# First two units of a convolved feed-forward taken tile by tile, squares added on VectorE, one column sum inside the third unit

## The chip, the cores and the metric

One NeuronCore of one Trainium2 chip runs the kernel. The metric is the device time of one execution in microseconds (us); the median of three runs of the kernel before is 2436.14 us.

## What is computed

A sequence of 512 tokens of width 1024 goes through two blocks. The first has a feed-forward, a gated linear attention mixer, a cross attention and a second feed-forward. The second adds 16 meta tokens (528 rows in all) and has two layers: an attention mixer or a pooling mixer, each followed by a feed-forward with a convolution over tokens. The change touches only how these two convolved feed-forwards begin. Cut to that:

```python
def rmsnorm(x, g):
    xf = x.astype(jnp.float32)
    y = xf * lax.rsqrt(jnp.mean(xf * xf, axis=-1, keepdims=True) + NORM_EPS)
    return (y * g.astype(jnp.float32)).astype(x.dtype)

def conv_ffn(h, w_up, conv_w, conv_b, w_down):
    L = h.shape[1]
    u = h @ w_up
    up = jnp.pad(u, ((0, 0), (CONV_WIDTH - 1, 0), (0, 0)))
    u = conv_b + sum(conv_w[j] * up[:, j:j + L] for j in range(CONV_WIDTH))
    gate, val = jnp.split(u, 2, axis=-1)
    return (jax.nn.silu(gate) * val) @ w_down

    # in each of the two layers, m being the mixer's output:
    h = h + rmsnorm(m, norm_mix_post[i])
    f = conv_ffn(rmsnorm(h, norm_ffn_pre[i]), ffn_w_up[i], ffn_conv_w[i], ffn_conv_b[i], ffn_w_down[i])
    h = h + rmsnorm(f, norm_ffn_post[i])
```

## The kernel before, in words

**Layout.** Activations lie transposed: the width of 1024 is KD = 8 tiles of 128 partitions, and the tokens are columns. X holds the residual, M the output of a mixer or feed-forward (8 tiles of 528 columns, free once it has been added to X). A number is split for TensorE into a high and a low part (XHI and XLO; w_hi and w_lo for weights).

**Units.** All weights are a flat list of units, numbered through the program. A unit of a feed-forward's first matrix is one output tile: for each of the 8 input tiles three products (lines 549, 551, 553), each in two column halves of 264 (258 in the second layer, which works on 516 columns), summed in one of four pairs of PSUM banks, pair n mod 4. A unit passes four engines: SP loads it into one of RAW = 4 slots, ACT copies it to w_hi in two halves (line 495, act_hi), POOL subtracts to get w_lo in two halves (line 482), PE multiplies. There are only SPLIT = 2 slots of w_hi and w_lo, so ACT takes unit n+2 only after PE has summed unit n, and PE starts each half of a unit only when POOL has done it (lo_done).

**The order of work** is written out by hand, one program for each engine, and the engines meet at semaphores. Before each convolved feed-forward, cffn0 and cffn1, stands a step called post (dve_post, act_post): for each tile k VectorE scales M by gain and norm (line 971), adds it to X (line 975) and later computes XLO (line 649), ACT computes XHI (line 638) and the square of X (line 644) into one of two buffers sq. In the loop of dve_post the XLO of tile k-3 follows the scaling of tile k.

**The norm of the feed-forward** needs the sum over all 1024 rows of the squares. In the kernel before TensorE forms it: pe_first_unit runs the first unit one tile at a time, as XLO arrives, and after each tile multiplies the tile's squares with a matrix of ones (pe_square, line 571) into the free bank pair n+3. From the sum VectorE makes ms (line 693), ACT takes a logarithm and an exponential (lines 675 and 676, with a table load before each), VectorE refines them in three steps (680 to 682) into rn, and only then can it read the first unit out of PSUM (line 915).

**ACT's order at the start of a feed-forward** (act_ffn, up, with it = 0, a = 0) matters for what follows:

```python
                    soon = blk > 1 and first(it) and pi == 0 and a == 0
                    look(it, n, 2 * a, count)
                    if first(it) and pi == 0 and a == 0:
                        act_sqrt(act, s, w)
                    act.wait_ge(unit_read, later(n, it, 2 * a + 1))
                    ...
                        nc.scalar.activation(g_conv[:, 0:w], g_buf[:, 2:2 + w], ACT.Identity, scale=tap(inv - 2, 2, f),
                                             bias=tap(inv - 2, 3, f)).then_inc(conv_tap, 1)
                        if soon:
                            look(it, n, 2 * a + 1, count)
```

The first look prepares unit n+2. Then come the root, the wait until VectorE has read unit n, and the convolution's first tap (line 861); the second look, which prepares unit n+3, stands behind them. The text below counts the units of a feed-forward from 0: unit 0 and unit 1 are prepared before it starts, unit 2 by the first look, unit 3 by the second.

## Time and profile before

| what | value |
|---|---|
| time, three runs | 2435.87, 2436.14, 2441.85 us, median 2436.14 |
| profiled execution, first to last instruction (span) | 2434.0 us |
| profiled execution, its own device time | not listed; the median is 2.1 us above the span |
| PE busy | 2298.1 us (94%) |
| DVE, ACT, POOL busy | 1082.2 us (44%), 910.5 us (37%), 981.7 us (40%) |
| mean granted clock of TensorE | 0.975 of full speed |
| step post and start of cffn0 | from 1534 to 1579 us of the span |
| step post and start of cffn1 | from 2011 to 2055 us of the span |

Engines: PE is TensorE's matmuls, DVE VectorE, ACT ScalarE, POOL GpSimd. Times within the profile are us from the span's start. A row of a timeline gives start, length, engine, line, output and inputs, how many instructions it merges and, in brackets, how long the engine had been idle and who released it. A clock of 1.00 is 2.4 GHz and one of 0.50 is 1.2 GHz. One matmul of the program for the column sum of squares shows as two records.

### The profile page before, as it was taken

How to read it: one execution, taken by the hardware profiler on the slowest of the kernel's cores; microseconds unless marked ns; L12 is line 12 of the kernel's file. 1: busy time of each engine (PE TensorE's matmuls, PEld its weight loads, DVE VectorE, ACT ScalarE, POOL GpSimd, SP SyncE). 2: the span in 40 equal slices, each digit the busy share in tenths (PEclk: the TensorE clock that was granted, in tenths of full speed). 3: DMA queues.
4: the chain of work that ended last, by engine and by line, in shares of the span. 5: the costliest groups of instructions: out<-in, count | busy, mean ns of one | idle time of the engine just before them, and what ended most of it. 6: DMA issues, size and time to landing. Idle time of an engine off the chain costs nothing.

```text
span 2434.0 us, 35964 instructions
## 1 busy us (share of the span) xinstructions
PE 2298.1 (94%) x14071; PEld 2016.9 (83%) x14071; DVE 1082.2 (44%) x1611; ACT 910.5 (37%) x1657; POOL 981.7 (40%) x751
## 2 busy tenths in 40 slices
PE   8999999999889899999998999799999958999999
PEld 6888887777677678888887888799999947999999
DVE  4313135565432243231466663562644486626354
ACT  4323235313343242232355443542433355424243
POOL 3445454532363244444451112244444412444443
PEclk9999999999899999999999999899999978999999
DMA  5333323321242123333221011133323211333321
GB/s 151 95 96 93 95 84 93 87 70 35 87 138 70 44 86 95 95 95 95 80 80 29 24 36 53 49 90 92 91 87 93 73 44 39 92 90 93 91 86 68
DMA packets 355686, 193.61 MB, mean 80 GB/s; under 512 B 7358, under 2 KB 350035, under 8 KB 355555
## 3 DMA queue, kind: packets, MB, share of 16 engines
q1 hardware_dynamic: 355026, 190.61, 27.0%
q8 instruction: 90, 1.47, 0.3%
q10 hardware_dynamic: 528, 1.19, 0.2%
q14 instruction: 42, 0.34, 0.0%
HBM read 189.67 MB, written 2.10 MB: 79 GB/s over the span
## 4 chain that ended last, share of the span: by engine, by line
PE 82%; DVE 12%; ACT 4%; issue 2%; DMA 0%; DVEq 0%; ACTq 0%; SPq 0%; POOL 0%
PE PS L549 22%; PE PS L551 22%; PE PS L553 22%; PE PS L2029 2%; PE PS L571 1%; PE PS L2047 1%; DVE u_conv L920 1%; PE PS L2101 1%; PE PS L2083 1%; ACT w_hi L495 1%; DVE g_conv L920 1%; DVE XLO L649 1%; DVE hid L931 1%; PE PS L1579 1%; DVE u_conv L923 1%
## 5 line engine op out<-in xcount | busy, mean ns | idle before, releaser
L482 POOL TENSOR_TENSOR w_lo<-raw,w_hi 128x512 fp32r<-128x512 f32 (+4 forms) x743 | 977.6, 1337 | 1430.4 <-ACT w_hi L495 1430.4
L549 PE MATMUL PS<-XHI,w_hi 128*128 128x512 f32 (+2 forms) x2632 | 738.9, 331 | 33.5 <-DVE XLO L649 29.3
L495 ACT ACTIVATE w_hi<-raw 128x512 fp32r<-128x512 f32 (+4 forms) x743 | 412.5, 603 | 929.9 <-PE PS L553 864.6
L551 PE MATMUL PS<-XLO,w_hi 128*128 128x512 f32 (+2 forms) x2632 | 730.5, 328 | 0.0
L553 PE MATMUL PS<-XHI,w_lo 128*128 128x512 f32 (+2 forms) x2632 | 728.3, 327 | 0.0
L549 PEld LDWEIGHTS PS<-XHI,w_hi 128*128 128x128 f32 x2632 | 445.9, 190 | 88.3 <-issue 36.3
L551 PEld LDWEIGHTS PS<-XLO,w_hi 128*128 128x128 f32 x2632 | 444.0, 190 | 45.7 <-issue 2.6
L553 PEld LDWEIGHTS PS<-XHI,w_lo 128*128 128x128 f32 x2632 | 444.7, 190 | 43.3
L549 PE MATMUL PS<-h_hi,w_hi 128*128 128x512 f32 (+2 forms) x1056 | 281.7, 321 | 6.0 <-DVE h_lo L933 5.8
L551 PE MATMUL PS<-h_lo,w_hi 128*128 128x512 f32 (+2 forms) x1056 | 281.7, 321 | 0.0
L553 PE MATMUL PS<-h_hi,w_lo 128*128 128x512 f32 (+2 forms) x1056 | 281.5, 321 | 0.0
L549 PEld LDWEIGHTS PS<-h_hi,w_hi 128*128 128x128 f32 x1056 | 175.4, 189 | 23.7 <-issue 6.3
L553 PEld LDWEIGHTS PS<-h_hi,w_lo 128*128 128x128 f32 x1056 | 175.7, 189 | 15.3
L551 PEld LDWEIGHTS PS<-h_lo,w_hi 128*128 128x128 f32 x1056 | 175.2, 188 | 15.5
L915 DVE TENSOR_TENSOR u_buf<-PS,rn 128x512 f32<-128x512 f32 (+2 forms) x88 | 61.2, 695 | 229.6 <-PE PS L553 229.6
L876 ACT ACTIVATE h_hi<-hid 128x512 fp32r<-128x512 f32 (+5 forms) x88 | 56.0, 636 | 207.7 <-DVE hid L931 207.7
L915 DVE TENSOR_TENSOR g_buf<-PS,rn 128x512 f32<-128x512 f32 (+2 forms) x88 | 61.0, 694 | 98.2 <-PE PS L553 97.8
L933 DVE TENSOR_TENSOR h_lo<-hid,h_hi 128x512 f32 (+5 forms) x88 | 68.9, 783 | 73.7 <-ACT h_hi L876 73.7
L920 DVE SCALAR_TENSOR_TENSOR u_conv<-u_buf,cols,u_conv 128x528 f32<-128x528 f32 (+1 forms) x44 | 71.4, 1624 | 65.7 <-ACT u_conv L873 65.7
L948 DVE SCALAR_TENSOR_TENSOR X<-PS,X 128x512 f32<-128x512 f32 x48 | 33.2, 691 | 148.6 <-PE PS L553 148.6
L920 DVE SCALAR_TENSOR_TENSOR g_conv<-g_buf,cols,g_conv 128x528 f32<-128x528 f32 (+1 forms) x44 | 54.8, 1246 | 47.4 <-ACT g_conv L861 47.4
L571 PE MATMUL PS<-sq,const 128*128 128x264 f32 (+2 forms) x144 | 50.0, 483 | 24.5 <-ACT sq L644 24.5
(311 smaller groups left out, 2371.5 us busy)
## 6 DMA issues: line engine op xcount, KB each, us to landing
raw<-in_ffn_w_up SPq DMA_DIRECT2D x132, 512.0 KB, 3.8
raw<-in_ffn_w_down SPq DMA_DIRECT2D x64, 512.0 KB, 4.0
raw<-in_ffn_w_gate SPq DMA_DIRECT2D x44, 512.0 KB, 3.9
raw<-in_w_in SPq DMA_DIRECT2D x25, 512.0 KB, 3.8
raw<-in_ffn_w_down SPq DMA_DIRECT2D x32, 384.0 KB, 3.4
raw<-in_xattn_w_kv SPq DMA_DIRECT2D x16, 512.0 KB, 3.8
raw<-in_w_out SPq DMA_DIRECT2D x8, 512.0 KB, 3.8
raw<-in_xattn_w_q SPq DMA_DIRECT2D x8, 512.0 KB, 3.8
```

The lines of the kernel that those rows point to most:

```text
L482: ins = nc.gpsimd.tensor_tensor(d, r, h.bitcast(F32), ALU.subtract)
L495: ins = nc.scalar.activation(d, r, ACT.Copy)
L549: nc.tensor.matmul(ps, wh, ahi(k)[:, c:c + w], start=(k == 0), stop=False)
L551: nc.tensor.matmul(ps, wh, alo(k)[:, c:c + w], start=False, stop=False)
L553: ins = nc.tensor.matmul(ps, wl, ahi(k)[:, c:c + w], start=False, stop=(k == u.kt - 1))
L571: ins = nc.tensor.matmul(ps, ones, sq[:, k % 2, c:c + w], start=(k == 0), stop=(k == KD - 1))
L876: nc.scalar.activation(h_hi[:, a + 2 * it, 0:w], hid[:, 0:w], ACT.Copy).then_inc(hid_hi, 1)
L915: nc.vector.tensor_tensor(sv(dst, blk), psv(m % 4, blk), r, ALU.mult).then_inc(unit_read, 1)
L920: nc.vector.scalar_tensor_tensor(cv_[:, 0:w], buf[:, 1:1 + w], tap(inv - 2, 1, ft), cv_[:, 0:w], ALU.mult, ALU.add).then_inc(conv_mid, 1)
L933: nc.vector.tensor_tensor(h_lo[:, a + 2 * it, 0:w], hid[:, 0:w], h_hi[:, a + 2 * it, 0:w].bitcast(F32), ALU.subtract).then_inc(hid_lo, 1)
L948: nc.vector.scalar_tensor_tensor(xt(m, 1), ps, 0.5, xt(m, 1), ALU.mult, ALU.add).then_inc(unit_read, 1)
L2029: ins = nc.tensor.matmul(bank[:, 0:CW], w, x[:, k, c * CW:(c + 1) * CW], start=st, stop=sp_)
```

## The change

- In cffn0 and cffn1, TensorE no longer sums the squares. pe_first_pair runs units 0 and 1 together: for each tile, as its XLO arrives, the six matmuls of unit 0 and the six of unit 1.
- pe_third_unit runs the first four tiles of unit 2, then the column sum of acc (pe_norm, one pass over the already added squares), then the other four tiles.
- ACT writes the eight squares into M, tile by tile, where the output has been used up; it no longer waits for a buffer sq.
- VectorE adds the eight squares in dve_square_tree: 4 tiles to 4 (2112 or 2064 columns), 2 to 2 (1056 or 1032), 1 to 1 (528 or 516), each waiting for the one before.
- dve_post has another order where a feed-forward follows: scale tile k, add tile k, XLO of tile k-1, so the addition waits for the scaling directly ahead of it.
- act_ffn, the weights' path and the other feed-forwards are as they were.

```diff
--- before.py
+++ after.py
@@ -585,6 +585,23 @@
         pe_unit(pe, n, 0, FLAT[n], lambda k: hi(k, blk), lambda k: lo(k, blk), outs_of(n % 4, blk), ready)
         pe_square(pe, s, pair, blk, KD - 1)
 
+    def pe_first_pair(pe, n, d, blk):
+
+        pe.wait_ge(unit_read, n)
+        for k in range(KD):
+            pe.wait_ge(x_lo, KD * d + k + 1)
+            for m in (n, n + 1):
+                pe_unit(pe, m, 0, FLAT[m], lambda k: hi(k, blk), lambda k: lo(k, blk), outs_of(m % 4, blk),
+                        signal=k == KD - 1, wait=False, ks=(k,))
+
+    def pe_third_unit(pe, n, s, blk):
+
+        for part in (range(0, KD // 2), range(KD // 2, KD)):
+            pe_unit(pe, n + 2, 0, FLAT[n + 2], lambda k: hi(k, blk), lambda k: lo(k, blk), outs_of((n + 2) % 4, blk),
+                    signal=part[0] > 0, wait=False, ks=part)
+            if part[0] == 0:
+                pe_norm(pe, s, (n + 3) % 4, blk).then_inc(norm_sum, 1)
+
     def step_link(eng, sm):
         n = [0]
 
@@ -598,7 +615,8 @@
     block = ctx.enter_context(nc.Block())
 
     S_FFN1, S_MIX, S_XAT, S_FFN2, S_FIN, S_MLA, S_MLAP, S_CF0, S_CF0P, S_POOL, S_POOLP, S_CF1, S_CF1P = range(13)
-    PE_SUMMED = (S_FFN1, S_CF0, S_POOL, S_POOLP, S_CF1)
+    PE_SUMMED = (S_FFN1, S_POOL, S_POOLP)
+    PAIRED = (S_CF0, S_CF1)
     D_FFN1, D_MIX, D_MIXO, D_XAT, D_XATO, D_FFN2, D_MLA, D_CF0, D_POOL, D_CF1 = range(10)
 
     OUT_ORDER = (1, 2, 3, 0)
@@ -800,6 +818,12 @@
             def up(it, n=n, pi=pi):
                 for j in range(4):
                     begin = first(it) and pi == 0
+                    if begin and j < 3 and s in PAIRED:
+                        if j == 0:
+                            pe_first_pair(pe, n, d, blk)
+                        if j == 2:
+                            pe_third_unit(pe, n, s, blk)
+                        continue
                     if begin and j == 0 and s in PE_SUMMED:
                         pe_first_unit(pe, n, s, d, blk, n)
                         continue
@@ -962,8 +986,28 @@
         pe.wait_ge(unit_read, n)
         pe_norm(pe, s, n % 4, 2).then_inc(norm_sum, 1)
 
-    def dve_post(dve, link, i, s, n, gain, d_next=None, g_next=None, blk_next=2):
+    def dve_square_tree(dve, link, s, w):
+
+        dve.wait_ge(sq_done, KD * (s + 1))
+        link(nc.vector.tensor_tensor(M[:, 0:4, 0:w], M[:, 0:4, 0:w], M[:, 4:8, 0:w], ALU.add))
+        link(nc.vector.tensor_tensor(M[:, 0:2, 0:w], M[:, 0:2, 0:w], M[:, 2:4, 0:w], ALU.add))
+        nc.vector.tensor_tensor(acc[:, 0:w], M[:, 0, 0:w], M[:, 1, 0:w], ALU.add).then_inc(acc_done, KD)
+
+    def dve_post(dve, link, i, s, n, gain, s_next, d_next=None, g_next=None, blk_next=2):
         dve_norm(dve, link, s, n % 4, 2)
+        if s_next in PAIRED:
+            for k in range(KD + 1):
+                if k < KD:
+                    if k >= 3:
+                        dve.wait_ge(post_added, KD * i + k - 2)
+                    nc.vector.scalar_tensor_tensor(post_t[:, k % 3, 0:S2], M[:, k, :], gain(k), rn[:, 0:S2], ALU.mult,
+                                                   ALU.mult).then_inc(post_scaled, 1)
+                    dve.wait_ge(post_scaled, KD * i + k + 1)
+                    nc.vector.tensor_tensor(X[:, k, :], X[:, k, :], post_t[:, k % 3, 0:S2], ALU.add).then_inc(post_added, 1)
+                if k:
+                    dve_split(dve, d_next, k - 1, blk_next, g_next)
+            dve_square_tree(dve, link, s_next, width(blk_next))
+            return
         for k in range(KD + 3):
             if k < KD:
                 if k >= 3:
@@ -983,7 +1027,10 @@
             act.wait_ge(post_added, KD * i + k + 1)
             if d_next is not None:
                 act_split(act, d_next, k, k, blk_next, g_next)
-            act_square(act, s_next, k, k, xt(k, blk_next), width(blk_next))
+            if s_next in PAIRED:
+                nc.scalar.activation(M[:, k, 0:width(blk_next)], xt(k, blk_next), ACT.Square).then_inc(sq_done, 1)
+            else:
+                act_square(act, s_next, k, k, xt(k, blk_next), width(blk_next))
 
 
 
@@ -2463,11 +2510,11 @@
         dve_ffn(dve, link, "ffn2", 1, 1, S_FFN2, lambda m, j: dve_fin_split(dve, m, j))
         dve_fin(dve, link)
         dve_mla(dve, link)
-        dve_post(dve, link, 0, S_MLAP, PHASE["mla"] + 26, G_POST[0], D_CF0, G_FPRE[0])
+        dve_post(dve, link, 0, S_MLAP, PHASE["mla"] + 26, G_POST[0], S_CF0, D_CF0, G_FPRE[0])
         dve_ffn(dve, link, "cffn0", 2, 2, S_CF0, lambda m, j: dve_acc(dve, S_CF0P, m, j, S2))
-        dve_post(dve, link, 1, S_CF0P, PHASE["cffn0"] + 68, G_FPOST[0])
+        dve_post(dve, link, 1, S_CF0P, PHASE["cffn0"] + 68, G_FPOST[0], S_POOL)
         dve_pool(dve, link)
-        dve_post(dve, link, 2, S_POOLP, 3, G_POST[1], D_CF1, G_FPRE[1], 3)
+        dve_post(dve, link, 2, S_POOLP, 3, G_POST[1], S_CF1, D_CF1, G_FPRE[1], 3)
         dve_ffn(dve, link, "cffn1", 3, 3, S_CF1, lambda m, j: dve_acc(dve, S_CF1P, m, j, S3))
         dve_out(dve, link)
```

PE at the start of cffn0 (L549, L551, L553 are the products, L571 the square's sum, L564 the column sum of acc; PS3 belongs to unit 0, PS0 to unit 1, PS1 to unit 2, PS2 to unit 3 and the norm). Before:

```order
L549 MATMUL PS3<-XHI,w_hi 128x264 [waits lo_done,x_lo,unit_read]
L549 MATMUL PS3<-XHI,w_hi 128x264
L551 MATMUL PS3<-XLO,w_hi 128x264 x2
L553 MATMUL PS3<-XHI,w_lo 128x264 x2
L571 MATMUL PS2<-sq,const 128x264 [waits sq_done]
L571 MATMUL PS2<-sq,const 128x264
L549 MATMUL PS3<-XHI,w_hi 128x264 [waits x_lo]
```

PE at the same place, with the change:

```order
L549 MATMUL PS3<-XHI,w_hi 128x264 [waits lo_done,x_lo,unit_read]
L549 MATMUL PS3<-XHI,w_hi 128x264
L551 MATMUL PS3<-XLO,w_hi 128x264 x2
L553 MATMUL PS3<-XHI,w_lo 128x264 x2
L549 MATMUL PS0<-XHI,w_hi 128x264 [waits lo_done]
L549 MATMUL PS0<-XHI,w_hi 128x264
L551 MATMUL PS0<-XLO,w_hi 128x264 x2
L553 MATMUL PS0<-XHI,w_lo 128x264 x2
L549 MATMUL PS3<-XHI,w_hi 128x264 [waits lo_done,x_lo]
```

After each tile of unit 0 stands the same tile of unit 1 where the square's sum stood. PE further on, with the change, at the column sum in the middle of unit 2:

```order
L553 MATMUL PS1<-XHI,w_lo 128x264 x2
L564 MATMUL PS2<-acc,const 128x264 [waits acc_done]
L564 MATMUL PS2<-acc,const 128x264
L549 MATMUL PS1<-XHI,w_hi 128x264 [waits lo_done]
L549 MATMUL PS1<-XHI,w_hi 128x264
L551 MATMUL PS1<-XLO,w_hi 128x264 x2
```

Behind it come four tiles of unit 2 and then unit 3, whose first row waits for lo_done, unit_read and norm_ms. VectorE in the post step ahead of cffn0 (the scaling writes post_t), before:

```order
L971 SCALAR_TENSOR_TENSOR post_t<-M,cols,rn 128x528 [waits post_added]
L975 TENSOR_TENSOR X<-X,post_t 128x528 [waits post_scaled]
L649 SCALAR_TENSOR_TENSOR XLO<-X,cols,XHI 128x528 [waits x_hi]
L975 TENSOR_TENSOR X<-X,post_t 128x528 [waits post_scaled]
L649 SCALAR_TENSOR_TENSOR XLO<-X,cols,XHI 128x528 [waits x_hi] x3
```

VectorE at the same place, the last tiles, with the change:

```order
L1003 SCALAR_TENSOR_TENSOR post_t<-M,cols,rn 128x528 [waits post_added]
L1006 TENSOR_TENSOR X<-X,post_t 128x528 [waits post_scaled]
L667 SCALAR_TENSOR_TENSOR XLO<-X,cols,XHI 128x528 [waits x_hi] x2
L992 TENSOR_TENSOR M<-M 128x2112 [waits sq_done]
L993 TENSOR_TENSOR M<-M 128x1056 [waits dve_step]
L994 TENSOR_TENSOR acc<-M 128x528 [waits dve_step]
```

Two XLO instead of three are left at the end, and the three adds follow. ACT at the start of cffn0, with the change; the rows are those of before but for line numbers and for the output of the last square, which was sq:

```order
L1031 ACTIVATE M<-X 128x528
L495 ACTIVATE w_hi<-raw 128x512 [waits unit_summed,raw_loaded1]
L495 ACTIVATE w_hi<-raw 128x512
L693 ACT_TABLE_LOAD
L693 ACTIVATE post_t<-ms 128x528 [waits norm_ms]
L694 ACT_TABLE_LOAD
L694 ACTIVATE post_t<-post_t 128x528 [waits act_step]
L885 ACTIVATE g_conv<-g_buf,cols 128x528 [waits unit_read]
L495 ACTIVATE w_hi<-raw 128x512 [waits unit_summed,raw_loaded2]
L495 ACTIVATE w_hi<-raw 128x512
```

The first pair of w_hi is unit 2, the second unit 3. Nothing moved here: unit 3's weights stand behind the whole norm in both kernels.

## Rows read from the trace of the kernel before

**Rows 1.** The page, part 4: the chain that ended last, by engine
```profile
PE 82%; DVE 12%; ACT 4%; issue 2%; DMA 0%; DVEq 0%; ACTq 0%; SPq 0%; POOL 0%
```

**Rows 2.** Timeline of PE, start of cffn0: start us, length us, idle before
```profile
1546.49 0.78 PE L549 MATMUL PS<-XHI,w_hi 128*128 128x264 f32 x2 [11.12 <-DVE XLO L649]
...
1559.20 0.60 PE L549 MATMUL PS<-XHI,w_hi 128*128 128x264 f32 x2
...
1560.12 1.05 PE L571 MATMUL PS<-sq,const 128*128 128x264 f32 x4
...
1560.82 0.60 PE L549 MATMUL PS<-XHI,w_hi 128*128 128x264 f32 x2
...
1561.73 0.40 PE L549 MATMUL PS<-XHI,w_hi 128*128 128x264 f32 x2
...
1578.61 0.41 PE L549 MATMUL PS<-XHI,w_hi 128*128 128x264 f32 x2
```

**Rows 3.** Timeline of DVE, same place
```profile
1540.26 0.71 DVE L682 SCALAR_TENSOR_TENSOR rn<-post_t 128x528 f32<-128x528 f32 x1
...
1541.00 1.45 DVE L971 SCALAR_TENSOR_TENSOR post_t<-M,cols,rn 128x528 f32<-128x528 f32 x2
...
1545.58 0.76 DVE L649 SCALAR_TENSOR_TENSOR XLO<-X,cols,XHI 128x528 fp32r<-128x528 f32 x1
...
1546.26 0.76 DVE L971 SCALAR_TENSOR_TENSOR post_t<-M,cols,rn 128x528 f32<-128x528 f32 x1
...
1547.56 0.76 DVE L649 SCALAR_TENSOR_TENSOR XLO<-X,cols,XHI 128x528 fp32r<-128x528 f32 x1
...
1561.28 0.71 DVE L693 TENSOR_SCALAR ms<-PS 128x528 f32<-128x528 f32 x1 [2.72 <-PE PS L571]
```

**Rows 4.** Timeline of ACT, same place
```profile
1560.38 1.15 ACT L495 ACTIVATE w_hi<-raw 128x512 fp32r<-128x512 f32 x2 [1.77 <-PE PS L553]
...
1569.19 1.14 ACT L495 ACTIVATE w_hi<-raw 128x512 fp32r<-128x512 f32 x2
```

**Rows 5.** Timeline of POOL, same place (a half is one instruction)
```profile
1561.09 1.29 POOL L482 TENSOR_TENSOR w_lo<-raw,w_hi 128x512 fp32r<-128x512 f32 x1 [25.88 <-ACT w_hi L495]
...
1569.88 1.36 POOL L482 TENSOR_TENSOR w_lo<-raw,w_hi 128x512 fp32r<-128x512 f32 x1 [6.25 <-ACT w_hi L495]
...
1576.91 2.55 POOL L482 TENSOR_TENSOR w_lo<-raw,w_hi 128x512 fp32r<-128x512 f32 x2 [3.95 <-ACT w_hi L495]
```

**Rows 6.** Start of cffn1, timelines: DVE twice, PE twice, POOL
```profile
2016.57 1.45 DVE L971 SCALAR_TENSOR_TENSOR post_t<-M,cols,rn 128x528 f32<-128x528 f32 x2
...
2037.66 0.70 DVE L693 TENSOR_SCALAR ms<-PS 128x516 f32<-128x516 f32 x1 [2.67 <-PE PS L571]
...
2022.05 0.77 PE L549 MATMUL PS<-XHI,w_hi 128*128 128x258 f32 x2 [11.18 <-DVE XLO L649]
...
2054.78 0.40 PE L549 MATMUL PS<-XHI,w_hi 128*128 128x258 f32 x2
...
2046.20 1.34 POOL L482 TENSOR_TENSOR w_lo<-raw,w_hi 128x512 fp32r<-128x512 f32 x1 [6.17 <-ACT w_hi L495]
```

**Rows 7.** Timeline of PE in the pooling stage: a start after a pause
```profile
2007.34 2.13 PE L571 MATMUL PS<-sq,const 128*128 128x264 f32 x4 [4.51 <-ACT sq L644]
```

**Rows 8.** Windows: length, busy PE, PEld, DVE, ACT, POOL, granted clock, DMA
```profile
1549.00:1550.00 1.00, 1.00 (x6) 0.85 (x5) 1.00 (x2) 0.16 (x1) 0.00 (x0) 0.72 0.00 0
...
2007.00:2008.00 1.00, 0.67 (x2) 0.56 (x3) 0.22 (x1) 0.98 (x3) 0.00 (x0) 0.50 0.00 0
...
2027.00:2028.00 1.00, 1.00 (x6) 0.85 (x5) 1.00 (x3) 0.00 (x0) 0.00 (x0) 0.78 0.00 0
...
795.00:805.00 10.00, 6.77 (x26) 3.98 (x26) 4.54 (x15) 4.32 (x14) 0.00 (x0) 1.00 0.00 0
```

**Rows 9.** Two lines, DVE and POOL: duration ns min/median/max
```profile
L2378 DVE TENSOR_TENSOR pb<-pa x4: 1290/1290/1291, 1978.9 to 2000.2; 128x1086 f32<-128x1086 f32 x4
...
L482 POOL TENSOR_TENSOR w_lo<-raw,w_hi x743: 378/1294/3280, 12.2 to 2410.8; 128x512 fp32r<-128x512 f32 x159, 128x384 fp32r<-128x384 f32 x16, 128x96 fp32r<-128x96 f32 x4, 128x576 fp32r<-128x576 f32 x4
```


## The prediction, made before the changed kernel ran

> **What bounds the kernel now.** I read the chain of waits first: TensorE carries 82% of it [rows 1], so a stretch is worth what it moves on TensorE. The change touches two stretches of some 45 us. There I read the engines' timelines side by side, then windows for the granted clock.
>
> The reader is to see three things at the start of cffn0. TensorE has been idle for 11.12 us when the first XLO arrives, works from 1546.49 without a pause, and begins unit 1 at 1560.82 and unit 4 at 1578.61 (units 1 to 3 are 24 tiles; 23 of them from 1561.73 give 0.734 us a tile) [rows 2]. The last square's sum begins at 1560.12, and VectorE forms ms at 1561.28, 1.16 us later [rows 2, 3]. I call that moment T. All that ACT does next hangs on T: the w_hi of unit 3 comes at 1569.19, T + 7.9, and its first w_lo half is ready at 1569.88 + 1.36 = 1571.24, T + 9.96 [rows 4, 5]. TensorE needs it only after 1560.82 + 16 tiles, at about 1572.7, for it has units 1 and 2 to do. So the norm is hidden behind two whole units with 1.5 us to spare. cffn1 is alike: T = 2037.66, unit 3's half ready at 2046.20 + 1.34 = 2047.54, T + 9.9; unit 4 at 2054.78, T + 17.1 [rows 6].
>
> **What the change removes.** Eight sums of squares a feed-forward. One costs 1561.73 - 1560.12 - 0.73 = 0.88 us of TensorE [rows 2], eight 7.0, and one column sum comes back: 6.2 us less work, twice. That is the hope; what follows is when the rest can run.
>
> **XLO's new pace.** VectorE's tile costs 1.98 us now (XLO to XLO, 1545.58 to 1547.56), of which scaling and addition take 1.30 (1546.26 to 1547.56) [rows 3]. In the new order the addition waits for the scaling just ahead. A dependent step starts 0.03 us after its forerunner's end (1540.26, 0.71 long, then 1541.00), an independent one 0.08 before it (0.76 long, next after 0.68) [rows 3]: 0.12 more, 2.10 us a tile. The first XLO needs two scalings and two additions, 2.84 us: it begins at 1541.00 + 2.84 = 1543.84, 1.7 us earlier than now. TensorE starts 0.15 after its end (now 1546.34, then 1546.49), at 1544.75. XLO of tile 6 begins at 1543.84 + 12.6 = 1556.44, that of tile 7 some 0.9 later.
>
> **The pair.** It costs 1.47 us a tile at full clock, less than the 2.10 of the supply, so the pair is bound by VectorE, with 0.6 us pauses. Tile 6 can start at 1557.35 and ends at 1558.82; tile 7 ends unit 0 at 1559.55 and the pair at 1560.3. Unit 1 is thus complete almost when it now begins. Does the clock bear the pauses? With TensorE 68% busy it was 1.00 for ten us [rows 8]; the pair is 70% busy. I take it that it holds.
>
> **Unit 2.** There are two weight slots, so unit 2's w_hi starts only 0.09 after unit 0: 1559.64 (now 1560.38, hidden by unit 1; then in the open). POOL follows 0.71 later and needs 1.29 [rows 4, 5], TensorE begins at 1561.74 after 1.4 us idle. Four tiles are 2.94: the column sum starts at 1564.68.
>
> **The adds.** 1086 columns take 1.29 us [rows 9], 528 take 0.71 [rows 3]: 1.04 ns a column, so 2112, 1056 and 528 columns take 2.36, 1.26 and 0.71, with two steps of 0.03 4.4 us. They start when XLO of tile 7 has been issued, 1558.0, and end at 1562.4. Cover: unit 2's first half, 2.3 us beyond. ACT's squares cost nothing: XHI and square take about 1.3 of each 2.10. The squares' place in M is used up.
>
> Here POOL and VectorE meet: POOL's w_lo of unit 2 is due at 1560.35, within the second add. The nearest row is POOL's own line, median 1294 ns, longest 3280 [rows 9]: an instruction can be held up by 2 us. From below the price is nothing, from above it is waiting until all adds end, 2.05 us. I take 0.2 a feed-forward, since the median says that most are hardly held.
> The Trainium skill ("SBUF — State Buffer", Who interferes with whom) says that a VectorE instruction with two SBUF inputs and a GpSimd instruction that reads SBUF exclude each other, and the second to issue blocks fully. By it the upper bound is the likelier one, and the sum below would be 3.7 higher; that is a rival.
>
> **T.** It comes at 1564.68 + 1.16 = 1565.84, 4.56 later than now. Everything in cffn1 hangs in the same way on its first scaling, at 2016.57 against 1541.00 [rows 3, 6]: T = 1565.84 + 475.57 = 2041.41, 3.75 later. (It is less, since TensorE started more slowly there before.)
>
> **Unit 3, the new wait.** After the column sum TensorE has only four tiles left: it is done at T - 1.16 + 0.88 + 2.94 = T + 2.7. Unit 3's weights still come at T + 9.96, so it starts at T + 10.06. That is 7.4 us idle where there was none, for ACT's second look stands behind root and first tap, unchanged. Then the clock: after a pause of 4.51 us it was 0.50 [rows 7, 8]. After the two long pauses it rose again at about 1549.6, 3.1 us after the start at 1546.49, and at about 2027.4, 5.4 us after 2022.05 (0.72 and 0.78 in those microseconds) [rows 2, 6, 8]. At half speed that loses 1.55 to 2.7 us. Unit 3 takes 5.87, so unit 4 starts at T + 17.5 to 18.6, where it now starts at T + 17.33 and T + 17.12. Its own weights are ready at 1576.91 + 1.28, T + 16.9 [rows 5]: hidden. From there on TensorE is continuous in both, and the shift stays.
>
> **Sum.** T later 4.56 + 3.75 = 8.3; unit 4 after T later by 0.15 to 1.3 and 0.3 to 1.4, middle 1.6; POOL 0.4: 10.3 us. On the profiled execution that is a span of 2434.0 + 10.3 = 2444.3. The median lies 2.1 above the span, so 2436.1 + 10.3 = **2446.4 us**, 0.42% slower. A measurement here can tell 0.3%, 7.3 us, from no change: 2443.4.
>
> **Rivals.**
> - *The adds hold POOL off.* Unit 2's w_lo starts after the last add, 2.05 later in each feed-forward, in place of the 0.2: 2446.4 + 3.7 = 2450.1. For: two engines on one memory, and a 3280 ns instruction. Against: the median. Chance 0.11.
> - *The mild case.* The dependent addition costs nothing (eight times 0.12, T earlier by 0.96, 1.9 in both) and the clock survives the 7.4 us pause (unit 4 at T + 17.0, by its weights: 2.0 less than the middle): 2446.4 - 3.9 = 2442.5, within 0.3%. Against: the dependent steps [rows 3] and the clock after a shorter pause [rows 7, 8]. Chance 0.10.
> - *TensorE's work decides, and it is faster.* If unit 3's weights were there when unit 2 ends, units 2 and 3 would run 1561.74 + 6.76 + 5.87 = 1574.4, unit 4 4.2 earlier than now, in cffn1 1574.37 + 475.57 against 2054.78, 4.8 earlier: 9.0 less, 2427.1. The point from which it decides: w_lo of unit 3 by T + 2.7 instead of T + 9.96. For: its slot is free at 1560.3, and TensorE does lose 12 us of work. Against: ACT's order. Chance 0.05.
>
> **How the numbers follow.** The forecast has the remaining 0.74, with its own range 2443.5 to 2449. The range for 8 in 10 takes in the mild case's end and part of the first rival: 2441.5 to 2450.5. Slower by over 0.3%: forecast and first rival, 0.85. Within: 0.10. Faster: 0.05.
>
> **What would show it.** In the changed profile: first product of cffn0 about 1.7 us earlier; XLO every 2.1 us; column sum at about 1564.7 with the adds done by then; ms 4.6 and 3.7 us later than now; a PE pause of 7 to 8 us before unit 3, released by w_lo, once in each feed-forward, with a clock of 0.50 behind it; POOL's next half at ms + 8.6. I am wrong if that pause is missing or under 3 us, if ms comes at 1562 or earlier, or if the end of cffn0 lies ahead of now.

## The result, and the profile after

The changed kernel takes 2451.09 us (median of 4 runs, 2446.24 to 2453.30) against 2438.10 us for the kernel before in the same measurement (4 runs, 2435.87 to 2441.85). The ratio is 1.0054 with a 95% interval of 1.0041 to 1.0066: slower, by 10 to 16 us. The direction was forecast, and so was the later T. The size was not, nor the path that leads from T to the end: 2446.4 was said, and 2451.09 lies 0.6 us beyond the range's upper end of 2450.5. Of the 4.7 us between the two, 2.0 belong to the kernel before, which took 2438.10 in this measurement where the prediction started from 2436.14. The other 2.7 are the change, 13.0 us in place of 10.3. The profiled execution took 2446.24 us with a span of 2444.4 us, against a span of 2434.0 before.

The page of the changed kernel, part 1 (busy us, share, instructions) and part 4 (the chain that ended last):

```profile
PE 2297.4 (94%) x14015; PEld 2016.6 (82%) x14015; DVE 1093.8 (45%) x1617; ACT 909.7 (37%) x1657; POOL 984.1 (40%) x751
...
PE 78%; DVE 14%; ACT 5%; issue 2%; DVEq 0%; POOL 0%; DMA 0%; ACTq 0%; SPq 0%
```

TensorE does fewer instructions and is busy almost as long as before (2298.1): what it was spared came back as work at a lower clock. From the first scaling to the pause in the second matrix the mean granted clock was 0.96 in cffn0 and 0.95 in cffn1, and is 0.91 and 0.93. In the chain its share fell from 82% [rows 1] to 78%, and VectorE and ACT together gained three points. Most of that fall says nothing of what the change costs: from 1749.8 to 1804.2 us, in the second half of cffn0, the chain now runs through ACT and VectorE where it ran through TensorE, though TensorE does not pause there in either kernel.

Timeline of PE at the start of cffn0, changed kernel, to be held against [rows 2]. The rows are: first product, first product of unit 2, column sum, first product of unit 3, of unit 4, and a start behind a pause in the second matrix.

```profile
1543.06 0.78 PE L549 MATMUL PS<-XHI,w_hi 128*128 128x264 f32 x2 [9.35 <-issue]
...
1561.19 0.56 PE L549 MATMUL PS<-XHI,w_hi 128*128 128x264 f32 x2 [2.39 <-POOL w_lo L482]
...
1565.74 1.05 PE L564 MATMUL PS<-acc,const 128*128 128x264 f32 x4
...
1576.14 0.78 PE L549 MATMUL PS<-XHI,w_hi 128*128 128x264 f32 x2 [6.43 <-POOL w_lo L482]
...
1584.68 0.40 PE L549 MATMUL PS<-XHI,w_hi 128*128 128x264 f32 x2
...
1662.92 0.48 PE L549 MATMUL PS<-h_hi,w_hi 128*128 128x264 f32 x2 [0.29 <-DVE h_lo L957]
```

Timeline of DVE there, against [rows 3]: two XLO, the three adds, ms (T):

```profile
1542.19 0.76 DVE L667 SCALAR_TENSOR_TENSOR XLO<-X,cols,XHI 128x528 fp32r<-128x528 f32 x1
...
1544.29 0.76 DVE L667 SCALAR_TENSOR_TENSOR XLO<-X,cols,XHI 128x528 fp32r<-128x528 f32 x1
...
1556.37 2.35 DVE L992 TENSOR_TENSOR M<-M 128x2112 f32<-128x2112 f32 x1
1558.76 1.26 DVE L993 TENSOR_TENSOR M<-M 128x1056 f32<-128x1056 f32 x1
1560.12 1.58 DVE L994 TENSOR_TENSOR acc<-M 128x528 f32<-128x528 f32 x1
...
1566.90 0.71 DVE L711 TENSOR_SCALAR ms<-PS 128x528 f32<-128x528 f32 x1 [5.05 <-PE PS L564]
```

Timeline of POOL, against [rows 5]: the first w_lo half of unit 2 and of unit 3.

```profile
1558.89 2.25 POOL L482 TENSOR_TENSOR w_lo<-raw,w_hi 128x512 fp32r<-128x512 f32 x1 [25.33 <-ACT w_hi L495]
...
1574.67 1.32 POOL L482 TENSOR_TENSOR w_lo<-raw,w_hi 128x512 fp32r<-128x512 f32 x1 [11.83 <-ACT w_hi L495]
```

Windows (columns as in [rows 8]), one microsecond each, behind the pause before unit 2 and behind the one before unit 3:

```profile
1562.00:1563.00 1.00, 1.00 (x6) 1.00 (x6) 0.00 (x0) 0.00 (x0) 0.84 (x1) 0.50 0.00 0
...
1576.50:1577.50 1.00, 1.00 (x6) 1.00 (x6) 0.68 (x2) 0.90 (x2) 1.00 (x1) 0.50 0.00 0
```

Start of cffn1, timelines of DVE (first scaling, ms) and PE (units 2 and 3, second matrix), against [rows 6]:

```profile
2021.51 0.77 DVE L1003 SCALAR_TENSOR_TENSOR post_t<-M,cols,rn 128x528 f32<-128x528 f32 x1
...
2048.65 0.69 DVE L711 TENSOR_SCALAR ms<-PS 128x516 f32<-128x516 f32 x1 [4.81 <-PE PS L564]
...
2043.19 0.80 PE L549 MATMUL PS<-XHI,w_hi 128*128 128x258 f32 x2 [2.35 <-POOL w_lo L482]
...
2057.79 0.77 PE L549 MATMUL PS<-XHI,w_hi 128*128 128x258 f32 x2 [6.36 <-POOL w_lo L482]
...
2143.65 0.48 PE L549 MATMUL PS<-h_hi,w_hi 128*128 128x258 f32 x2 [0.58 <-DVE h_lo L957]
```

**Where the 10.4 us of span came from.** In this execution cffn0 began 1.66 us earlier (first scaling 1539.34, before 1541.00), a difference from upstream, where nothing was changed. So I count from the first scaling. To T it is 27.56 us now and was 20.28; in cffn1 27.14 and 21.09. To the end of TensorE's pause in the second matrix, where it waits for VectorE's h_lo, it is 123.58 and was 117.19; in cffn1 122.14 and 116.95. In the trace of the kernel before the two pause ends are these rows of PE:

```profile
1658.19 0.48 PE L549 MATMUL PS<-h_hi,w_hi 128*128 128x264 f32 x2 [1.63 <-DVE h_lo L933]
...
2133.52 0.48 PE L549 MATMUL PS<-h_hi,w_hi 128*128 128x258 f32 x2 [1.75 <-DVE h_lo L933]
```

The two stretches grew by 6.39 and 5.19 us, together 11.6; less the 1.66 upstream, and with 0.5 behind the two stretches, that is the 10.4 of span. The runs differ by 13.0, interval 10 to 16; the rest is within that interval and has no place of its own.

**Which engine sets the end of the stretch.** I had read the chain on the page only, as shares of the whole span. Cut to this stretch, it says something else. The chain of the kernel before, from unit 2's weights to the second matrix:

```profile
1560.38 1.15 ACT w_hi L495 x2
1561.55 1.28 ACT L675
1562.85 0.65 ACT post_t L675
...
1570.12 1.70 DVE g_conv L923
...
1581.41 1.14 ACT w_hi L495 x2
...
1583.30 1.92 DVE u_conv L920
...
1658.19 0.48 PE PS L549 x2
```

Between 1560.38 and 1658.19 the chain has no piece of TensorE at all. It does not pass through ms either: ms ends at 1561.99 and the logarithm's table load only at 1562.83, since ACT first has unit 2's w_hi to write. So T had 0.8 us to spare in the kernel before. The chain of the changed kernel in the same place:

```profile
1565.90 0.90 PE PS L564 x4
1566.90 0.72 DVE ms L711
1567.64 0.65 ACT post_t L693
...
1574.91 1.66 DVE g_conv L947
...
1662.92 0.48 PE PS L549 x2
```

Here too nothing of TensorE stands between the column sum and the second matrix. From T on, the norm and eight rounds of convolution (each takes one unit of the gate and one of the value) run through ACT and VectorE, and that takes 96.02 us (before 96.91). TensorE's start of units 3 and 4 is no part of it. But it is not far from it: in the second matrix TensorE waited 1.63 us for h_lo before and waits 0.29 us now (1.75 and 0.58 in cffn1), so it was nearly the later of the two.

### The profile page after: what moved, and what is told of

It is laid out like the page before. It is cut to its first block, busy times and chain, and to the rows that moved or that the text cites. A ratio compares the mean times of both kernels' runs of the same rounds, so it can differ in the third digit from the quotient of the medians.

```text
span 2444.4 us, 35866 instructions
## 1 busy us (share of the span) xinstructions
PE 2297.4 (94%) x14015; PEld 2016.6 (82%) x14015; DVE 1093.8 (45%) x1617; ACT 909.7 (37%) x1657; POOL 984.1 (40%) x751
## 4 chain that ended last, share of the span: by engine, by line
PE 78%; DVE 14%; ACT 5%; issue 2%; DVEq 0%; POOL 0%; DMA 0%; ACTq 0%; SPq 0%
PE PS L549 21%; PE PS L551 21%; PE PS L553 21%; PE PS L2076 2%; DVE u_conv L944 2%; PE PS L2094 1%; ACT w_hi L495 1%; PE PS L2130 1%; PE PS L2148 1%; DVE XLO L667 1%; DVE g_conv L944 1%; PE PS L571 1%; DVE hid L955 1%; DVE u_conv L947 1%; DVE g_conv L947 1%
## 5 line engine op out<-in xcount | busy, mean ns | idle before, releaser
L549 PE MATMUL PS<-XHI,w_hi 128*128 128x512 f32 (+2 forms) x2632 | 740.6, 332 | 48.8 <-issue 18.8
L551 PE MATMUL PS<-XLO,w_hi 128*128 128x512 f32 (+2 forms) x2632 | 733.5, 329 | 0.0
L553 PE MATMUL PS<-XHI,w_lo 128*128 128x512 f32 (+2 forms) x2632 | 731.0, 329 | 0.0
L549 PEld LDWEIGHTS PS<-XHI,w_hi 128*128 128x128 f32 x2632 | 448.6, 192 | 104.6 <-issue 43.4
L551 PEld LDWEIGHTS PS<-XLO,w_hi 128*128 128x128 f32 x2632 | 447.6, 191 | 45.7 <-issue 2.6
L553 PEld LDWEIGHTS PS<-XHI,w_lo 128*128 128x128 f32 x2632 | 448.0, 192 | 43.1
L549 PE MATMUL PS<-h_hi,w_hi 128*128 128x512 f32 (+2 forms) x1056 | 281.7, 321 | 3.6 <-DVE h_lo L957 3.5
L551 PE MATMUL PS<-h_lo,w_hi 128*128 128x512 f32 (+2 forms) x1056 | 281.7, 321 | 0.0
L553 PE MATMUL PS<-h_hi,w_lo 128*128 128x512 f32 (+2 forms) x1056 | 281.4, 321 | 0.0
L549 PEld LDWEIGHTS PS<-h_hi,w_hi 128*128 128x128 f32 x1056 | 175.4, 189 | 21.3 <-issue 4.0
L553 PEld LDWEIGHTS PS<-h_hi,w_lo 128*128 128x128 f32 x1056 | 175.7, 189 | 15.3
L551 PEld LDWEIGHTS PS<-h_lo,w_hi 128*128 128x128 f32 x1056 | 175.2, 188 | 15.5
L2197 ACT ACTIVATE pt<-PS 128x640 f32<-128x640 f32 (+4 forms) x80 | 37.3, 471 | 87.2 <-PE PS L2130 86.2
```

The costliest lines, as they stand in the source:

```text
L549: nc.tensor.matmul(ps, wh, ahi(k)[:, c:c + w], start=(k == 0), stop=False)
L551: nc.tensor.matmul(ps, wh, alo(k)[:, c:c + w], start=False, stop=False)
L553: ins = nc.tensor.matmul(ps, wl, ahi(k)[:, c:c + w], start=False, stop=(k == u.kt - 1))
L2197: act_m.inc(nc.scalar.activation(pt[:, x % 4, 0:j + 1, 0:nq], turn_at(x).rearrange("p (i q) -> p i q", q=P)[:, :, 0:nq], ACT.Copy), ("tc", x))
```

## The experiments

Two explanations were to be told apart; the expectations call them theory A and theory B. A: what decides is T, since a fixed chain of ACT and VectorE follows it. B: what decides is TensorE's idle time and the half clock behind it, above all the 6.4 us before unit 3, which would then also be the place to mend. Beside them stood the size of T itself: the clock in unit 2, and POOL held up by the adds.

The table has T and the end of the pause in the second matrix, us from the first scaling, in cffn0 and cffn1, both from one profile; then what the two pause ends give against the kernel before (117.19 and 116.95); then what the timed ratio gives, as (ratio - 1) x 2438.

| kernel | T | pause end | the two stretches | ratio, 95% interval | timed |
|---|---|---|---|---|---|
| before | 20.28, 21.09 | 117.19, 116.95 | - | 1 | - |
| the change | 27.56, 27.14 | 123.58, 122.14 | +11.6 | 1.0054 [1.0041, 1.0066] | +13.2 |
| e1_w3 | 27.56, 27.31 | 122.42, 121.33 | +9.6 | 1.0037 [1.0024, 1.005] | +9.0 |
| e2_w34 | 27.57, 27.32 | 121.43, 120.37 | +7.7 | 1.0043 [1.0028, 1.0058] | +10.5 |
| e3_sum_first | 24.65, 24.02 | 120.48, 119.02 | +5.4 | 1.0032 [1.0021, 1.0044] | +7.8 |
| e4_one_unit | 23.71, 23.51 | 119.47, 118.44 | +3.8 | 1.0024 [1.0013, 1.0036] | +5.9 |
| e5_order | 19.90, 19.75 | 116.81, 115.61 | -1.7 | 0.999 [0.9981, 0.9999] | -2.4 |
| e6_fill3 | 27.56, 27.32 | 123.58, 122.23 | +11.7 | 1.0046 [1.0031, 1.0061] | +11.2 |
| e7_fill2 | 26.05, 25.83 | 121.88, 120.80 | +8.5 | 1.0032 [1.0021, 1.0044] | +7.8 |
| e8_one_add | 25.06, 24.89 | 120.85, 119.82 | +6.5 | 1.003 [1.002, 1.004] | +7.3 |
| e9_early_ln | 19.90, 19.75 | 116.04, 114.75 | -3.4 | 0.9991 [0.9982, 1.0] | -2.2 |
| e10_ln_silu | 19.89, 19.76 | 117.14, 115.74 | -1.3 | 1.0007 [0.9998, 1.0016] | +1.7 |
| e11_change | 27.56, 27.26 | 123.61, 122.20 | +11.7 | 1.0056 [1.0043, 1.007] | +13.6 |

The stretches repeat closely (the change and e11_change: T equal in cffn0, 0.12 apart in cffn1), the timed differences only to some 3 us. Both columns put the kernels in nearly the same order. So what follows rests on the stretches, with the timed column as a check.

**e1_w3.** Unit 3's w_hi comes ahead of the norm.

```diff
                     look(it, n, 2 * a, count)
+                    if soon:
+                        look(it, n, 1, count)
...
-                        if soon:
-                            look(it, n, 2 * a + 1, count)
```

> Unit 3's weights are converted by ACT ahead of the root instead of behind the first tap; all else as in the changed kernel. Theory A (everything that ACT and VectorE do hangs on the norm's moment T): the pause before unit 3 goes, but unit 4's weights still come at T + 16.2, so a pause of 7.5 us stands before unit 4 in its place, with the clock at half behind it; the time stays within 3 us of the changed kernel (2448 to 2454). Theory B (only unit 3's place in ACT's order is at fault): both pauses of 6.4 us go for good, 11 to 14 us less, about 2438.

The pause before unit 3 is gone, and one of 6.53 us stands before unit 4, whose first product comes 42.77 us after the first scaling instead of 45.34. By the second matrix the 2.6 us have shrunk to 1.16. And these 1.16 come mostly from elsewhere: the second g_conv step of VectorE (the 1.66 us piece in the chain above) is short here, since POOL's w_lo of unit 3 no longer runs beside it. The median, 2447.40, lies 0.6 us below theory A's band and far from theory B's 2438. Timeline of DVE in e1_w3:

```profile
1577.80 0.77 DVE L947 SCALAR_TENSOR_TENSOR g_conv<-g_buf,cols,g_conv 128x528 f32<-128x528 f32 x1
```

**e2_w34.** Units 3, 4 and 5 move up by one place in ACT's order.

```diff
+                    head = blk > 1 and first(it) and pi == 0
+                    look(it, n, 3 if head and a else 2 * a, count)
+                    if soon:
+                        look(it, n, 1, count)
...
-                            look(it, n, 2 * a + 1, count)
+                            look(it, n, 2, count)
...
-                    if not soon:
+                    if not head:
```

> As the run before, and the weights of units 4 and 5 are moved up one place as well. Theory A: a pause of at most 1 us before units 4 and 5, but unit 6's weights wait for the end of VectorE's second pair, T + 25.5, and come at T + 27.6 where TensorE wants them at T + 22; against the changed kernel, where unit 6 starts at T + 29.4, 0 to 4 us are won in both feed-forwards together: 2447 to 2451. Theory B: 12 us less or more, 2439 or below.

The long pause is broken up: 0.47 and 0.85 us before units 4 and 5, and 2.85 before unit 6. Another 1.0 us is saved in each stretch, as in e1 the difference from T to pause end, not T. The timed column doesn't show it (10.5 against 9.0, intervals overlapping). TensorE's long pause can be moved out of sight without the time following.

**e6_fill3.** Thirteen spare products keep TensorE at work in the pause before unit 3.

```diff
                         pe.wait_ge(norm_ms, s + 1)
+                        if s in PAIRED:
+                            for _ in range(13):
+                                nc.tensor.matmul(PS[(n + 3) % 4][:, 0, 0:264], ones, const[:, 0:264], start=True, stop=True)
```

> The changed kernel with 13 spare matmuls of ones by a constant in the pause ahead of unit 3, into the bank pair that unit 3 overwrites. If the clock's fall in that pause is what costs: the clock stays at 1.00, unit 3 is 2.1 to 2.4 us shorter, unit 4 starts at T + 16.1 by its weights, 1.3 to 1.7 us earlier in each: 3 us less than the changed kernel. If the chain behind T decides alone: 1 us less or none.

This is the cleanest test of the pause. Timeline of PE in e6_fill3, unit 3 and the second matrix (first scaling at 1545.22):

```profile
1582.03 0.48 PE L549 MATMUL PS<-XHI,w_hi 128*128 128x264 f32 x2 [0.64 <-POOL w_lo L482]
...
1668.80 0.48 PE L549 MATMUL PS<-h_hi,w_hi 128*128 128x264 f32 x2 [1.87 <-DVE h_lo L960]
```

The window behind the spare products:

```profile
1582.00:1583.00 1.00, 0.97 (x8) 1.00 (x9) 1.00 (x2) 0.81 (x2) 1.00 (x1) 1.00 0.00 0
```

The clock stays at 1.00 and unit 4 starts 1.7 us earlier (43.67 against 45.34). In the second matrix TensorE then waits 1.87 us where it waited 0.29, and goes on after 123.58 us as before. The price of the half clock behind the pause before unit 3 is nothing in the end.

**e7_fill2.** The same with five spare products in the pause before unit 2.

```diff
+        for _ in range(5):
+            nc.tensor.matmul(PS[(n + 3) % 4][:, 0, 0:264], ones, const[:, 0:264], start=True, stop=True)
         for part in (range(0, KD // 2), range(KD // 2, KD)):
```

> The changed kernel with 5 spare matmuls of ones by a constant in the pause of 2.4 us ahead of unit 2. If that pause makes the clock fall: it stays at 1.00, the first half of unit 2 takes 2.9 us instead of 4.6, T comes 1.6 us earlier in each feed-forward and all behind it: 3.3 us less. If the clock fell for the 70% busy pair ahead of it, the spare work comes too late and T stays at 27.5 us after the first scaling.

PE in e7_fill2, and its window behind the pause:

```profile
1559.91 2.39 PE L600 MATMUL PS<-const 128*128 128x264 f32 x10
1562.47 0.51 PE L549 MATMUL PS<-XHI,w_hi 128*128 128x264 f32 x2 [0.17 <-POOL w_lo L482]
```

```profile
1562.00:1563.00 1.00, 0.83 (x6) 0.53 (x5) 0.99 (x2) 0.00 (x0) 1.00 (x2) 1.00 0.03 8
```

Here the clock does pay, since the first half of unit 2 lies ahead of the column sum: T comes 1.51 and 1.31 us earlier, and the pause ends follow by 1.70 and 1.34. Two pauses, one remedy, opposite results: what tells them apart is on which side of T they lie.

**e8_one_add.** The second and third add are left out, so the norm in this kernel is made from an acc that does not hold these squares.

```diff
-        link(nc.vector.tensor_tensor(M[:, 0:4, 0:w], M[:, 0:4, 0:w], M[:, 4:8, 0:w], ALU.add))
-        link(nc.vector.tensor_tensor(M[:, 0:2, 0:w], M[:, 0:2, 0:w], M[:, 2:4, 0:w], ALU.add))
-        nc.vector.tensor_tensor(acc[:, 0:w], M[:, 0, 0:w], M[:, 1, 0:w], ALU.add).then_inc(acc_done, KD)
+        nc.vector.tensor_tensor(M[:, 0:4, 0:w], M[:, 0:4, 0:w], M[:, 4:8, 0:w], ALU.add).then_inc(acc_done, KD)
```

> The changed kernel without the second and third add of the squares (the norm is then made from what acc held; that part of the computation is left out). If the adds hold POOL off: the first w_lo half of unit 2 takes 1.3 us instead of 2.2, unit 2 starts 0.9 us earlier, the pause ahead of it is 1.5 us, and T comes at least 0.9 us earlier in each: 2 us less, and 5 us less if the shorter pause leaves the clock up. If not, nothing moves.

POOL and PE in e8_one_add:

```profile
1562.05 2.51 POOL L482 TENSOR_TENSOR w_lo<-raw,w_hi 128x512 fp32r<-128x512 f32 x2 [25.33 <-ACT w_hi L495]
...
1563.37 0.51 PE L549 MATMUL PS<-XHI,w_hi 128*128 128x264 f32 x2 [1.41 <-POOL w_lo L482]
```

With no add beside it POOL makes both halves in 2.51 us (3.95 with the change, of which the first half took 2.25). The pause is 1.41 us instead of 2.39, 1.0 shorter, and behind it the clock is still 1.00:

```profile
1564.00:1565.00 1.00, 1.00 (x11) 1.00 (x10) 0.00 (x0) 0.00 (x0) 0.55 (x1) 1.00 0.00 0
```

T comes 2.50 us earlier: 1.0 of it is POOL's, and 1.5 is the clock that did not fall. In cffn1 it is 2.25. The two adds themselves were covered, as forecast; it was their neighbours that paid. And T without them, 25.06 and 24.89 us after the first scaling, is the prediction's 24.84 to 0.2 us.

**e3_sum_first.** The column sum ahead of unit 2 instead of inside it.

```diff
-        for part in (range(0, KD // 2), range(KD // 2, KD)):
...
-            if part[0] == 0:
-                pe_norm(pe, s, (n + 3) % 4, blk).then_inc(norm_sum, 1)
+        pe_norm(pe, s, (n + 3) % 4, blk).then_inc(norm_sum, 1)
+        pe_unit(pe, n + 2, 0, FLAT[n + 2], lambda k: hi(k, blk), lambda k: lo(k, blk), outs_of((n + 2) % 4, blk), wait=False)
```

> The column sum is made ahead of unit 2 instead of in its middle; ACT's order as in the changed kernel. Theory A: T comes 3.5 us earlier in each feed-forward, the pause before unit 3 shrinks to about 2 us, unit 4 starts 5 us earlier in each: 9 to 11 us less than the changed kernel, about 2441. Theory B: the pause before unit 3 still has the same cause, and T moves by 3.5 us: 7 us less, 2444.

TensorE now waits 2.95 us for the adds and T is 2.9 and 3.1 us earlier; the stretches follow by 3.10 and 3.12. The half unit put ahead of the column sum had cost more than the wait that it filled. The column sum itself is slow here, 2.13 us for four records that take 1.05 with the change:

```profile
1563.56 2.13 PE L564 MATMUL PS<-acc,const 128*128 128x264 f32 x4 [2.95 <-DVE acc L991]
```

Both theories had promised more than the 6.2 us that the two stretches gave: theory A 9 to 11 us, since unit 4 would start 5 us earlier, theory B 7. Unit 4 does start 4.6 and 4.1 us earlier, and only T's 2.9 and 3.1 arrive at the second matrix. Here too unit 4's start is not what counts.

**e4_one_unit.** Unit 0 alone tile by tile, and the column sum inside unit 1.

```diff
-            for m in (n, n + 1):
+            for m in (n,):
...
-                    if begin and j < 3 and s in PAIRED:
+                    if begin and j < 2 and s in PAIRED:
...
-                        if j == 2:
-                            pe_third_unit(pe, n, s, blk)
+                        if j == 1:
+                            pe_split_unit(pe, n, 1, s, blk)
```

> Only unit 0 is taken tile by tile; the column sum stands in the middle of unit 1, units 2 and 3 are whole; VectorE's order and adds as in the changed kernel. Theory A: unit 1 covers unit 2's weights again, T lies 23.5 us after the first scaling (20.3 before, 27.5 with the change), pause before unit 3 about 1 us: 10 us less than the changed kernel and 2 to 4 us more than before, about 2441. Rival (the pair itself is the gain, and undoing it costs TensorE time): slower than the changed kernel, 2453 or more.

Unit 1 hides unit 2's weights again, the column sum waits 0.43 us for the adds, and T comes 3.85 and 3.63 earlier than with the change. It is still 3.4 and 2.4 later than before. So the adds cost time even where the pair is gone: none of them can run before the last square is there, and the column sum had to wait for them, where before the sum of the last square stood right behind the last tile. Against e5 below, which shares VectorE's order and leaves the sums to TensorE, T is 3.8 us later in both feed-forwards.

**e5_order.** The kernel before with nothing of the change but VectorE's new order in the post step.

```diff
         dve_norm(dve, link, s, n % 4, 2)
+        if d_next is not None:
+            for k in range(KD + 1):
...
+                if k:
+                    dve_split(dve, d_next, k - 1, blk_next, g_next)
+            return
```

> The kernel before with one part of the change alone: VectorE's new order in the post step ahead of both convolved feed-forwards (scale, add, XLO of the tile before). TensorE sums the squares as before, unit 0 alone is taken tile by tile. Theory A (only the moment T of the norm decides): the last XLO ends 17.1 us after the first scaling, T comes at 19.2 us instead of 20.3 and 21.1, unit 4 starts 1 and 2 us earlier: 3 us less than before, about 2435. Rival (the slower pace of 2.10 us a tile costs what the earlier start gives): 2438, as before.

T is 0.38 and 1.34 us earlier (1.1 and 1.9 were expected), the time 0.999 with an interval that ends at 0.9999. It is the one part of the change that helps, and a small one. With e4 this splits the change's delay of T, 7.28 and 6.05 us, into three parts: the new order takes 0.38 and 1.34 off, adds and column sum bring 3.81 and 3.76, and the pair, with unit 2's weights behind it, 3.85 and 3.63.

**e9_early_ln.** e5 and, ahead of unit 2's weights, a logarithm of one column, which brings the table load of the logarithm forward.

```diff
+                    if soon:
+                        act_link(act, nc.scalar.activation(sd[:, 0:1], ones[:, 0:1], ACT.Ln))
                     look(it, n, 2 * a, count)
```

> The new order alone (as in the run before with TensorE's sums), and ACT takes the logarithm of one column of ones ahead of unit 2's weights, so that the table load of 1.28 us lies ahead of T. If all that follows hangs on T and on the length of the chain behind it: the table load leaves the chain, the pause of TensorE at the first unit of the second matrix ends 115.9 and 114.7 us after the first scaling (116.8 and 115.6 with the order alone, 117.2 and 117.0 before): 1.7 us less than with the order alone, 3.5 less than before, about 2434.5. If TensorE's own work bounds the stretch: its start of that unit does not move, 2436.

ACT in e9_early_ln; T is at 1564.86:

```profile
1561.83 1.28 ACT L856 ACT_TABLE_LOAD   x1
1563.12 0.20 ACT L856 ACTIVATE post_t<-const 128x1 f32<-128x1 f32 x1
1563.97 1.15 ACT L495 ACTIVATE w_hi<-raw 128x512 fp32r<-128x512 f32 x2 [0.65 <-PE PS L553]
1565.60 0.65 ACT L675 ACTIVATE post_t<-ms 128x528 f32<-128x528 f32 x1 [0.47 <-DVE ms L693]
```

The logarithm follows ms without a load between them, and the pause ends come 0.77 and 0.86 earlier than in e5, with T the same. In the changed kernel this happened by itself: the load ran from 1559.35 to 1560.63, while ACT waited for the late T. That accounts for its T-to-end distance of 96.02 in place of 96.91. Against the kernel before, e9 measures 0.9991, interval 0.9982 to 1.0, and so no better than e5 in what can be told.

**e10_ln_silu.** e9 with unit 3's w_hi behind the first SiLU instead of ahead of it.

```diff
-                        if soon:
-                            look(it, n, 2 * a + 1, count)
...
-                    if not soon:
-                        look(it, n, 2 * a + 1, count)
+                    look(it, n, 2 * a + 1, count)
```

> As e9, and unit 3's weights are converted behind the first SiLU instead of ahead of it. By the chain: the SiLU comes up to 0.9 us earlier since POOL no longer holds up VectorE's tap, the pause at the second matrix ends up to 0.9 us earlier still in each feed-forward, though TensorE waits about 1 us for unit 3: 0 to 1.8 us less than e9. By TensorE's work: 2 us more than e9.

This missed: 1.10 and 0.99 us are lost instead of gained. DVE and POOL in e10_ln_silu:

```profile
1572.02 1.91 DVE L919 SCALAR_TENSOR_TENSOR u_conv<-u_buf,cols,u_conv 128x528 f32<-128x528 f32 x1 [1.86 <-ACT u_conv L872]
```

```profile
1570.83 2.55 POOL L482 TENSOR_TENSOR w_lo<-raw,w_hi 128x512 fp32r<-128x512 f32 x2 [7.70 <-ACT w_hi L495]
```

The g_conv step is now short (0.77 us). But w_hi stands in ACT's order between SiLU and u_conv, and uses up that gain: u_conv's first VectorE step starts 31.15 us after the first scaling, in e9 31.13. And that step takes 1.91 us in place of 0.77, since POOL's w_lo now runs beside it: 1.14 us, the whole loss in cffn0.

**e11_change.** The changed kernel once more, on another occasion, with nothing edited.

> The changed kernel as it was, on the same chip as the two others: T 27.6 and 27.1 us after the first scaling again, 12 to 14 us more than before, about 2451.

2452.32 us (5 runs) against 2437.07, ratio 1.0056 [1.0043, 1.007]. The result stands.

## Why the prediction was right and wrong

**Right.** Kernel slower, and by a later T. XLO every 2.10 us (said: 2.10) and the first of them 2.85 after the scaling (2.84). The adds 2.35 and 1.26 us (2.36 and 1.26). Unit 2's weights in the open, with a pause; the clock at 1.00 through the pair's short pauses from 1548 us on; the column sum not waiting for the adds; a pause before unit 3 in each feed-forward, released by w_lo, of 6.43 and 6.36 us (7.4), with a clock of 0.50 behind it. Unit 4 at 1584.68, T + 17.78, and in cffn1 at T + 17.42 (17.5 to 18.6). "TensorE's work decides" was rightly given little: TensorE was spared 6.2 us twice and nothing of it came through.

**The step that failed** is the term for POOL: "I take 0.2 a feed-forward, since the median says that most are hardly held". With that term T would have come 25.0 us after the first scaling; 27.56 and 27.14 were measured. In cffn0 T, said to come at 24.84 without the term, comes apart so. Unit 2's w_lo started 0.20 later than worked out. It took 2.25 us instead of 1.29. And the first half of unit 2 took 1565.74 - 1561.19 = 4.55 us instead of 2.94: 1.61. Together with 0.05 less elsewhere that is 2.72. The last two are one cause and its effect, as e8 shows:
- *POOL itself.* It was 1.0, not 0.2. A median over 743 instances says what happens to most, not what happens to the one that falls due inside an add. The Trainium skill ("SBUF — State Buffer", Who interferes with whom) has the rule that the second of the two to issue blocks fully, and the rows agree to within 0.2 us if it is read instruction by instruction: POOL, issued at 1558.89, waited for the end of the second add (1558.76 + 1.26 = 1560.02) and was done 1.12 us after it, at 1561.14 (1.29 is its time alone); the third add, issued at 1560.12, then took 1.58 us where 0.71 is its own. I had made the upper bound from all the adds in a row, but POOL got its turn between two of them.
- *The clock behind it*, the larger part. The sentence "I take it that it holds" was about the pair, and the steps behind it carried it over a pause of 1.4 us before unit 2. So far it was right: with a pause of 1.41 us the clock stayed at 1.00 (e8). POOL's delay made 2.39 us of that pause, and then the clock fell to 0.50. e7 gives the price: 1.51 us of T in cffn0 and 1.31 in cffn1. The prediction priced POOL's delay as a shift only and did not ask what a longer pause does to the clock.

So POOL's collision cost 2.50 and 2.25 us of T in place of 0.2.

**The path behind T** was wrong as well, and made the miss smaller, not larger. "So the norm is hidden behind two whole units" looked only at when TensorE wants unit 3, and "from there on TensorE is continuous in both, and the shift stays" made unit 4's start the end of the account. The chain from the norm to the second matrix runs through ACT and VectorE, and TensorE's wait of 1.63 us for h_lo in the trace of the kernel before shows it.

**Errors that cancelled.** I priced unit 4's start after T at +1.6 us for both, and it was worth nothing (e6, e1, e3). I did not see that a later T hides the table load, 0.9 in each. By the steps: T + 8.3, unit 4 + 1.6, POOL + 0.4 made 10.3; measured in the stretches, T + 7.28 + 6.05 = 13.3, POOL within it, less 1.8 for the table load, 11.5, against 11.6 from the pause ends. That 10.3 lies as near to it as it does is luck. Behind both errors is one reading: "TensorE carries 82% of it, so a stretch is worth what it moves on TensorE". That share is of the whole span. In the stretch at stake TensorE's share of the chain is nil, and the chain cut to the window would have shown this before any run.

**The rivals.** The mild case is out: the dependent addition costs its 0.12, and the clock fell. The first rival was right on the cause, and its 2.05 us a feed-forward lie near the 2.50 and 2.25 measured. But it had POOL wait for all the adds, and POOL waited for one: half of its mechanism came true, and the clock, which it did not name, made up the rest.

**Why the squares were better on TensorE.** In the kernel before they cost it 7.0 us of work, but without them unit 0 waits for XLO: with VectorE's order the same, unit 1 starts 19.43 and 19.29 us after the first scaling with the eight sums (e5) and 18.93 and 18.62 without them (e4). So 7.0 us of work moved unit 1 by 0.50 and 0.67. And the last sum stood 1.16 us ahead of ms. The change trades time that TensorE has to spare in this stretch for time ahead of T, which nothing covers.

**Open.** Between 1.5 and 2 us of the timed difference have no place (11.6 in the stretches, 13.2 and 13.6 timed), and are no more than the interval allows. No version tried beats the kernel before by an amount that is certain to be more than the measurement's 0.3%; e5 and e9, the best, are at 0.1%.

## What to carry to other kernels

Cut the chain of waits to the stretch that is changed, before pricing anything by the engine that leads it over the whole program. In these runs a pause of TensorE cost time only ahead of what that chain hangs on: the same remedy was worth 1.5 us in front of the norm's sum and nothing behind it. That holds as long as the other engine has slack, and here it had 0.29 us left. Price a collision of POOL and VectorE by the instruction that falls due inside the other's, not by the median of its line, and then ask what the longer pause does to TensorE's clock: the delay itself was 1.0 us and its echo in the clock 1.5.

## What the runs showed of the hardware that was not expected

- The clock after a short pause. From 1543.06 to 1558.8 TensorE was fed tile by tile, with short gaps, and then had nothing. After 1.41 us it came back at 1.00 and stayed there (e8). After 2.39 us the clock fell to 0.50 some 0.3 us behind the restart (the change, cffn0). After the 2.95 us of e3 it was at 0.50 when the column sum began. With the gap filled but for 0.17 us it stayed at 1.00 (e7), although the spare products did no useful work.
- VectorE and POOL hold each other up in both directions. A w_lo half of 1.29 us took 2.25 behind an add. A convolution step of 0.77 us took up to 1.92 with w_lo beside it. Who gets the next turn is not always the one that waits: POOL got in between two adds that stood 0.10 us apart, but in e10 the u_conv step, begun at 1572.02, was held through the rest of one w_lo half (to 1572.12) and all of the next (to 1573.37). In the chain of the kernel before, seven steps of u_conv in cffn0's first eight rounds are 1.80 to 1.92 us long, over 7 us in that stretch alone. Whether another order could take them out was not tried; e10 shows one that only moves the collision.
